# State-space steps of a hybrid encoder block: time-step matrices and squares on ScalarE, normalization one step late, the diagonal's second term in the skip weight

## The reference, cut to what matters

```python
xdt = xh * dt[..., None]
cs = jnp.cumsum(dt * a, axis=2)                      # inside a chunk of 128
seg = cs[:, :, :, None] - cs[:, :, None, :]
decay = jnp.where(mask, jnp.exp(jnp.where(mask, seg, 0.0)), 0.0)   # mask: lower triangle with diagonal
cb = jnp.einsum('bcqgn,bcsgn->bcqsg', cc, bc)
y_diag = jnp.einsum('bcqsgh,bcsghp->bcqghp', cb[..., None] * decay, xdt)
...
y = y_f + y_b + xh * d_skip[:, None]
y = y.reshape(bsz, l, SSD_INNER) * jax.nn.silu(z)
y = y.reshape(bsz, l, SSD_GROUPS, SSD_INNER // SSD_GROUPS)
y = y * lax.rsqrt(jnp.mean(y * y, -1, keepdims=True) + RMS_EPS)    # over 384 columns
y = y.reshape(bsz, l, SSD_INNER) * norm_g
return y @ w_out
```

## Time and profile before

| what | value |
|---|---|
| median of three runs | 2252.95 us (2252.62 to 2254.93) |
| profiled execution, its own time | 2250.3 us |
| its span, first to last instruction | 2248.3 us |
| busy over the span: PE, DVE, ACT, POOL | 1995.2, 674.6, 328.2, 314.7 us |
| mean granted TensorE clock | 0.94 of full |
| Sqrt of step 0 starts, Sqrt of step 14 starts | 485.20 us, 666.42 us |
| mix stage begins on TensorE | 672.70 us |

### The profile page before, as it was taken

How to read it: one execution, slowest core, us unless ns; L and a number is a source line. 1 busy time by engine, 2 the same in 40 slices (tenths; PEclk the granted TensorE clock), 3 DMA queues, 4 the chain that set the end, 5 groups by cost and what they waited for, 6 DMA issues and landing times.

```text
span 2248.3 us, 19706 instructions
## 1 busy us (share of the span) xinstructions
PE 1995.2 (89%) x8321; PEld 938.4 (42%) x8321; DVE 674.6 (30%) x1075; ACT 328.2 (15%) x547; POOL 314.7 (14%) x278
## 2 busy tenths in 40 slices
PE   8996899998979999598889889879889888988987
PEld 4664544455554444433334334334334333333332
DVE  6599965589970112300000000000000000000002
ACT  1433212144450001100000000000000000000001
POOL 2866600066640000000000000000000000000001
PEclk9898999999989999699999999999989999999999
DMA  5531221110013218389999999999999999999995
GB/s 138 126 107 26 66 96 69 39 52 28 29 57 131 84 66 351 122 341 427 429 428 424 428 428 425 431 426 427 429 427 427 428 426 427 428 427 426 427 428 228
DMA packets 86887, 625.45 MB, mean 278 GB/s; under 512 B 21036, under 2 KB 34576, under 8 KB 57616
## 3 DMA queue, kind: packets, MB, share of 16 engines
q1 hardware_dynamic: 74400, 616.41, 66.8%
q10 hardware_dynamic: 12400, 7.79, 1.2%
HBM read 614.39 MB, written 9.78 MB: 278 GB/s over the span
## 4 chain that ended last, share of the span: by engine, by line
PE 47%; DMA 28%; DVE 9%; ACT 2%; issue 1%; SPq 0%; DVEq 0%; ACTq 0%
PE ps L843 47%; DMA arena<-in_w_e 28%; ACT arena L568 1%; DVE arena L1598 1%; DVE arena L1546 1%; ACT L568 1%; DVE arena L1602 1%; DVE arena L1573 1%; DVE arena L1603 1%; DVE arena L1571 1%; DVE arena L1599 0%; DVE arena L1590 0%; DVE arena L1678 0%; DVE arena L1595 0%; DVE arena L1689 0%
## 5 line engine op out<-in xcount | busy, mean ns | idle before, releaser
L843 PE MATMUL ps<-arena 128*64 128x512 f32 (+7 forms) x7786 | 1927.6, 534 | 213.8 <-DMA arena<-in_w_e 114.5
L843 PEld LDWEIGHTS ps<-arena 128*64 128x64 f32 (+2 forms) x7786 | 877.4, 164 | 1247.8 <-issue 1062.5
L568 ACT ACTIVATE arena<-ps 128x512 f32<-128x512 f32 (+5 forms) x286 | 161.8, 597 | 1697.3 <-PE ps L843 898.2
L1698 DVE TENSOR_TENSOR arena<-arena,ps 128x512 f32<-128x512 f32 (+1 forms) x48 | 30.3, 645 | 581.5 <-PE ps L843 581.5
L560 POOL TENSOR_TENSOR arena<-arena 128x1024 f32<-128x1024 f32 x3 | 7.1, 2355 | 1324.8 <-ACT arena L568 1324.8
L1707 DVE TENSOR_TENSOR arena<-arena,ps 128x512 f32<-128x512 f32 x48 | 33.1, 690 | 338.5 <-PE ps L843 338.5
L568 ACT ACT_TABLE_LOAD x71 | 91.1, 1283 | 23.8 <-issue 21.4
L568 ACT ACTIVATE arena<-arena 64x512 f32<-64x512 f32 (+6 forms) x138 | 62.8, 513 | 164.2 <-DVE arena L1603 93.5
L1531 DVE SCALAR_TENSOR_TENSOR arena<-arena 128x512 f32<-128x512 f32 x80 | 62.5, 781 | 2.8
L1689 DVE TENSOR_TENSOR arena<-arena 128x512 f32<-128x512 f32 x8 | 5.6, 694 | 182.4 <-PE ps L1260 181.4
L544 POOL TENSOR_TENSOR arena<-arena 128x768 f32<-128x768 f32 x16 | 24.3, 1522 | 171.6 <-PE ps L1004 134.1
(11 more groups left out here) (180 smaller groups left out, 769.7 us busy)
## 6 DMA issues: line engine op xcount, KB each, us to landing
arena<-in_w_e SPq DMA_DIRECT2D x128, 2816.0 KB, 28.9
arena<-in_w_e SPq DMA_DIRECT2D x80, 2048.0 KB, 28.5
arena<-in_w_in SPq DMA_DIRECT2D x9, 2048.0 KB, 8.6
arena<-in_w_e SPq DMA_DIRECT2D x16, 1024.0 KB, 30.6
arena<-in_w_in SPq DMA_DIRECT2D x5, 1536.0 KB, 6.4
arena<-in_w_out_ssd SPq DMA_DIRECT2D x4, 1536.0 KB, 6.7
gate_scratch<-arena ACTq DMA_DIRECT2D x16, 256.0 KB, 2.4
arena<-gate_scratch SPq DMA_DIRECT2D x4, 1024.0 KB, 8.0
```

What stands on the lines that cost most here:

```text
L568: return act.activation(out, in_, func, **kw)
L843: return pe.matmul(out, lhsT, rhs, start=a, stop=z)
L1698: tt(o, o, ps[:, i, 0:w], ALU.mult).then_inc(s.hid_ready, 1)
```

## The change

Four things are done at once. (a) The time-step matrix is made by ScalarE in dt_matrix: per head one Identity of 128x128 of the mask m_gt, with scale dt_b - dt_f (dt_step, made once) and bias dt_f, both read per partition; so each side of the diagonal has its own time step and the diagonal has dt_f alone. It is double-buffered. GpSimd's three operations of a step go. (b) The missing dt_b on the diagonal is moved into the skip weight: GpSimd multiplies B and C elementwise once per group (bc_prod), TensorE sums it over the state with a column of ones (128x1 result in bank 4), and VectorE makes diag_x = dt_b * that + d_row (128x6), which replaces d_row in the skip term. (c) The squares are taken by ScalarE (Square with accum_out), and its Sqrt follows. (d) VectorE's reciprocal and scaling of step i-1 stand in step i, behind mixing_matrix(i+1).

```diff
--- before.py
+++ after.py
@@ -182,13 +182,14 @@
             return ctx.enter_context(nc.semaphore(name))
 
 
-        C = Space(arena, 0, 2300)
+        C = Space(arena, 0, 2440)
         ident, eps_col = C.take(P), C.take(1)
         late_at = C.at
         m_le, m_gt, m_ge, m_lt, ones = (C.take(P) for _ in range(5))
         chunk_no = C.take(NC)
         conv_w, conv_b = C.take(XBC // P, CONV), C.take(XBC // P)
         dt_bias, a_neg = C.take(2 * HEADS), C.take(2 * HEADS)
+        dt_step, diag_x = C.take(TT, HEADS), C.take(2, HG)
         d_row, norm_g = C.take(HEADS), C.take(INNER // P)
         dtime = C.take(TT, 2 * HEADS)
         da, w_end, e_cs, e_all = (C.take(TT, 2 * HEADS) for _ in range(4))
@@ -260,9 +261,10 @@
         cacc = S2.take(4, SEQ)
         xc = S2.take(4, SEQ)
         S = Space(arena, S.at, top)
-        dmat, uf, emat, gmat = S.take(HG, P), S.take(HG, P), S.take(HG, P), S.take(2, HG, P)
+        dmat, emat, gmat = S.take(2, HG, P), S.take(HG, P), S.take(2, HG, P)
         S = Space(arena, S2.at - 4 * SEQ, top)
         rhs_f, rhs_b = S.take(HG, P), S.take(HG, P)
+        bc_prod = S.take(SEQ)
 
 
         S = Space(arena, late_at, top)
...
@@ -538,18 +540,15 @@
             for i in range(GROUPS * TT):
                 g, c = divmod(i, TT)
                 f, b = slice(HG * g, HG * g + HG), slice(HEADS + HG * g, HEADS + HG * g + HG)
+                if c == 0:
+                    pool.wait_ge(s.silu_done, 17 + g)
+                    if g >= 1:
+                        pool.wait_ge(s.cb_ps, i)
+                    pool.tensor_tensor(bc_prod, bT[:, g, :], cT[:, g, :], ALU.mult).then_inc(s.bc_ready, 1)
                 if i >= 1:
-                    pool.wait_ge(s.mats_ready, 2 * i)
                     pool.wait_ge(s.segm_ps, i)
                 pool.tensor_tensor(rhs_f, first(m_le, HG), last(da[:, c, f], P), ALU.mult)
                 pool.tensor_tensor(rhs_b, first(m_ge, HG), last(da[:, c, b], P), ALU.mult).then_inc(s.mats_ready, 1)
-                if i == 0:
-                    pool.wait_ge(s.silu_done, 20)
-                if i >= 1:
-                    pool.wait_ge(s.g_ready, i)
-                pool.tensor_tensor(uf, first(m_le, HG), last(dtime[:, c, f], P), ALU.mult)
-                n.link(pool.tensor_tensor(dmat, first(m_ge, HG), last(dtime[:, c, b], P), ALU.mult))
-                pool.tensor_tensor(dmat, dmat, uf, ALU.add).then_inc(s.mats_ready, 1)
 
             pool.wait_ge(s.wo_ps, 2 * TT)
             pool.iota(slot_no, pattern=[[1, CAP]], base=1, channel_multiplier=0,
@@ -717,6 +716,21 @@
                     act.wait_ge(s.g_ready, i)
                 f(emat.rearrange("p (a b) q -> p a (b q)", a=2), ps[:, 2:4, 0:GI], ACT.Exp).then_inc(s.segm_exp, 1)
 
+            def dt_matrix(i):
+
+                g, c = divmod(i, TT)
+                if i >= 2:
+                    act.wait_ge(s.g_ready, i - 1)
+                for j in range(HG):
+                    h0 = HG * g + j
+                    r = f(dmat[:, i % 2, j, :], m_gt, ACT.Identity, scale=dt_step[:, c, h0:h0 + 1], bias=dtime[:, c, h0:h0 + 1])
+                r.then_inc(s.dmat_ready, 1)
+
+            def root(i):
+                act.wait_ge(s.gate_ready, i + 1)
+                n.link(f(ty[:, 0], ty[:, 3], ACT.Square, accum_out=rms[:, i % 2, 0:1]))
+                f(rms[:, i % 2, 1:2], rms[:, i % 2, 0:1], ACT.Sqrt, scale=1.0 / GI, bias=eps_col).then_inc(s.rms_sqrt, 1)
+
             def y_copied(i):
 
                 g, c = divmod(i, TT)
@@ -725,20 +739,23 @@
                     f(yT[:, 3 * g + j, P * c:P * c + P], ps[:, 1, P * j:P * (j + 1)], ACT.Copy,
                       scale=norm_g[:, 3 * g + j:3 * g + j + 1]).then_inc(s.yt_copied, 1)
 
+            act.wait_ge(s.conv_done, 20)
+            dt_matrix(0)
             z_gate(0, 0)
             decays(0)
             for c in range(1, Z_AHEAD):
                 z_gate(0, c)
+            dt_matrix(1)
             for i in range(GROUPS * TT):
                 g, c = divmod(i, TT)
                 if i + 1 < GROUPS * TT:
                     decays(i + 1)
                 if i >= 1:
                     y_copied(i - 1)
-                act.wait_ge(s.gate_ready, i + 1)
-                f(rms[:, i % 2, 1:2], rms[:, i % 2, 0:1], ACT.Sqrt, scale=1.0 / GI, bias=eps_col).then_inc(s.rms_sqrt, 1)
+                root(i)
                 if i + Z_AHEAD < GROUPS * TT:
                     z_gate(*divmod(i + Z_AHEAD, TT))
+                    dt_matrix(i + Z_AHEAD)
                 elif c == TT - 2:
 
                     act.wait_ge(s.yT5_loaded, 16)
@@ -1027,8 +1044,10 @@
                 q = slice(P * c, P * c + P)
                 if i >= 1:
                     pe.wait_ge(s.g_ready, i)
+                pe.wait_ge(s.bc_ready, g + 1)
+                mm(ps[:, 4, P:P + 1], bc_prod[:, q], ones[:, 0:1], True, True)
                 mm(ps[:, 4, 0:P], bT[:, g, q], cT[:, g, q], True, True).then_inc(s.cb_ps, 1)
-                pe.wait_ge(s.mats_ready, 2 * i + 1)
+                pe.wait_ge(s.mats_ready, i + 1)
                 if i >= 1:
                     pe.wait_ge(s.segm_exp, i)
                 for a in range(2):
@@ -1508,6 +1527,7 @@
                 if q == 0:
                     dve.wait_ge(s.seg_exp, 1)
                     n.done(tt(w_end, w_end, dtime, ALU.mult))
+                    n.done(tt(dt_step, dtime[:, :, HEADS:], dtime[:, :, 0:HEADS], ALU.subtract))
                 toeplitz_rows(q)
                 for d in range(2):
                     recur(q, d)
@@ -1568,9 +1588,21 @@
                 if i >= 2:
                     dve.wait_ge(s.yd_ps, i - 1)
                 o = gmat[:, i % 2]
+                g, c = divmod(i, TT)
+                n.done(stt(diag_x[:, i % 2], dtime[:, c, HEADS + HG * g:HEADS + HG * g + HG], ps[:, 4, P:P + 1],
+                           d_row[:, HG * g:HG * g + HG], ALU.mult, ALU.add))
                 n.link(tt(o, emat, first(ps[:, 4, 0:P], HG), ALU.mult))
-                dve.wait_ge(s.mats_ready, 2 * i + 2)
-                tt(o, o, dmat, ALU.mult).then_inc(s.g_ready, 1)
+                dve.wait_ge(s.dmat_ready, i + 1)
+                tt(o, o, dmat[:, i % 2], ALU.mult).then_inc(s.g_ready, 1)
+
+            def normalized(i):
+
+                dve.wait_ge(s.rms_sqrt, i + 1)
+                n.link(dve.reciprocal(rms[:, i % 2, 2:3], rms[:, i % 2, 1:2]))
+                if i >= 1:
+                    dve.wait_ge(s.yt_ps, i)
+                ts(ty[:, 4], ty[:, 3], rms[:, i % 2, 2:3], None, ALU.mult).then_inc(s.yn_ready, 1)
+                dve.wait_ge(s.yn_ready, i + 1)
 
             for j in range(TT - 1):
                 weighted_x(0, j)
@@ -1586,8 +1618,10 @@
                     weighted_x(g + 1, c)
                 if i + 1 < GROUPS * TT:
                     mixing_matrix(i + 1)
+                if i >= 1:
+                    normalized(i - 1)
                 y0, y1, y2 = ty[:, 0], ty[:, 1], ty[:, 2]
-                n.done(tt(h3(y0), h3(xs[:, c, gi]), bc(d_row[:, f]), ALU.mult))
+                n.done(tt(h3(y0), h3(xs[:, c, gi]), bc(diag_x[:, i % 2]), ALU.mult))
                 dve.wait_ge(s.yd_ps, i + 1)
                 if c >= 1:
                     n.done(tt(h3(y1), h3(ps[:, 6, 0:GI]), bc(e_cs[:, c, f]), ALU.mult))
@@ -1599,17 +1633,10 @@
                 tt(y0, y0, ps[:, 5, 0:GI], ALU.add).then_inc(s.y_read, 1)
                 dve.wait_ge(s.y_read, i + 1)
                 dve.wait_ge(s.z_silu, g * TT + c + 1)
-                n.link(tt(ty[:, 3], y0, zg[g % 2][:, c], ALU.mult))
-                dve.tensor_tensor_reduce(out=y0, in0=ty[:, 3], in1=ty[:, 3], scale=1.0, scalar=0.0, op0=ALU.mult, op1=ALU.add,
-                                         accum_out=rms[:, i % 2, 0:1]).then_inc(s.gate_ready, 1)
+                tt(ty[:, 3], y0, zg[g % 2][:, c], ALU.mult).then_inc(s.gate_ready, 1)
                 if more:
                     carry(g + 1, c)
-                dve.wait_ge(s.rms_sqrt, i + 1)
-                n.link(dve.reciprocal(rms[:, i % 2, 2:3], rms[:, i % 2, 1:2]))
-                if i >= 1:
-                    dve.wait_ge(s.yt_ps, i)
-                ts(ty[:, 4], ty[:, 3], rms[:, i % 2, 2:3], None, ALU.mult).then_inc(s.yn_ready, 1)
-                dve.wait_ge(s.gate_ready, i + 1)
+            normalized(GROUPS * TT - 1)
 
             dve.wait_ge(s.sg_loaded, 64)
             for hf in range(2):
```

More of the change, by code:

```diff
@@ L307, in encoder @@
         pool_step m_cleared maps_cleared xbc_ps xbc_raw conv_done silu_done nat_ps nat_copied z_ps z_silu
-        xw_ready st_ps carried cb_ps segm_ps segm_exp mats_ready g_ready yd_ps y_read gate_ready rms_sqrt
+        xw_ready st_ps carried cb_ps segm_ps segm_exp mats_ready dmat_ready bc_ready diag_ready g_ready yd_ps y_read gate_ready rms_sqrt
         yn_ready yt_ps yt_copied mix_ps mix_sig mix_read glu_done mix_ready mixT_ps mixT_copied wo_ps wo_read
```

## The result

The changed kernel takes 2289.33 us in the median (2287.83 to 2291.05, four runs) against 2252.78 of the kernel before: a ratio of 1.0161, with a 95% interval of 1.0145 to 1.0177. It is 36.5 us slower. The forecast was 18.6 slower, 2271.6, with a range up to 2286: the direction was right, the size half of what was measured, and the time lies outside the range.

What follows compares the result with a forecast made beforehand. ScalarE and VectorE handing one token back and forth bound the steps. Intervals +22.2, start -5.5, end +1.9 give +18.6 us on 2250.3, so 2268.9; plus 2.65 to the median, 2271.6 us, range 2258 to 2286.

Steps and rivals of the forecast that it cites:

- ScalarE's section: ScalarE's work from VectorE's gate_ready to the mixing matrix's start; claimed to grow from 4.32 to 8.3 us.
- The table load: Load for the Sqrt, now behind the Square and hence behind ScalarE's wait; claimed to enter the chain at 1.28 us.
- a sign against it: Named disproof in ScalarE's list: Identities taking over 0.45 or under 0.25 us each.
- My 0.07 for an operand: Cost in us of each per-partition operand of a ScalarE Identity, giving six Identities 2.05 us.
- VectorE's part: VectorE's work from mixing matrix to gate_ready: 6.55 us in chunks 1 and 2, 5.5 in chunks 0 and 3.
- TensorE's round: From L1596 to the next L1596 via transposes, z_tile, states, scores and GpSimd's pair: 14.75 us with added states, 13.4 without.
- The sum of the intervals: The 14 gate-to-gate intervals of the steps together: 203.4 us claimed against 181.2 before, +22.2.
- The circle: ScalarE and VectorE waiting on each other, gate to gate: 14.85 us eight times and 13.8 six times.
- TensorE's term: Extra from TensorE and GpSimd behind chunk 0 of groups 1 and 2: 0.9 us each, 1.8 together.
- TensorE's clock: Rival: new waits before TensorE's transposes drop z_tile to 1.2 GHz; three cases give 2287 us; chance 0.14.
- the upper bound of (3): Six Identities on ScalarE at 0.44 us each, without overlap: 2.6 us instead of 2.05.
- Start and end: Before step 0, 5.5 us gained; behind step 14, 1.9 us lost to Square and table load before the mix stage.

Runs made afterwards that it cites:

- filler run: Changed kernel plus three unused 384-column products on TensorE per step, just before it waits for the normalization: 2271.42 us, ratio 1.0082.

## Why the prediction was wrong

Set side by side, the medians make a ladder from before to after: time-step matrix and diagonal term with the Identities in ScalarE's wait, 2226.7 (two parts of the change at once, which no run separates); Identities in the section instead, 2244.9 (+18.2); squares on ScalarE, 2260.7 (+15.8); late normalization, 2289.3 (+28.7). The steps depend on their order: the last one costs 43.5 on the kernel of 2226.7, and 48 in the kernel before.

- *ScalarE's section.* Right in the main: 8.3 forecast, 8.5 measured. The table load came into the chain as read from the order. The Identities were 2.41 for six, not 2.05: each took 0.483 and followed the last by 0.39. By duration that is over the 0.45 which the prediction named as a sign against it, by pace it is not. My 0.07 for an operand came from a copy that reads PSUM and a form that reads SBUF. Both read SBUF in the Identity with two operands (0.483) and the 64x128 form with none (0.299): 0.09 for each, an estimate, as the forms differ in their partitions. The 93 ns and the some 2.3 us by the Trainium skill (ScalarE: Activation LUTs, "What ACT_TABLE_LOAD costs"), which I did not take, were nearer.
- *VectorE's part.* 7.0 and 5.7 (5.9 in chunk 3) against 6.55 and 5.5, by the filler run's chain. VectorE's products of y took 0.6 us and less, as forecast. diag_x was sized at 0.15; it takes 0.23 alone, but 0.65 in the mean, as it has two inputs in SBUF and falls under the lock, which I had tied to L1596 only.
- *The step that failed* is the one in the prediction's words: "Against ScalarE's 14.85 and 13.8 this decides only behind chunk 0 of groups 1 and 2 (14.75 against 13.8), 0.9 us each." TensorE's round was seen, but sized at full clock, 14.75 and 13.4, and so looked harmless next to the section. Its wait before the transposes was put at 1 to 2 us; it was 1.8 to 3.7. Behind ten of the 13 waits up to 686 us four to eight rows ran at half speed, some 0.3 us each. The round became 16 us and decided in most steps. The whole late normalization adds 28.4 us to the intervals (195.4 without it): 14.6 are the clock, as the filler run shows, and 13.8 are almost all VectorE's part, 0.85 to 1.1 us in most steps where 0.68 was charged.
- *The sum of the intervals, term by term.* The circle was put at 201.6 (118.8 + 82.8) and is 209.2 by the filler run: section and VectorE's part were too small by 7.6 together. TensorE's term was put at 1.8 and is 14.6, all of it gone when the clock is back. Together these are the 20 us between 203.4 and 223.75.
- *The rival "TensorE's clock"* named this and got 0.14, with "three such cases"; the clock was under 0.98 in all 14 intervals. The mistake is in the weighing: the rival was priced by how rarely it showed before, where TensorE waited for L1599 10 times, and not by the fact that the change makes the wait a fixed part of each round. The range had a slip too: the upper bound of (3) with two falls of 5.33 each comes to some 2290, not 2286.
- *A maximum of two circles at full clock* is not what a step does. In the changed kernel the weight loads waited for the scaling 13 times up to 686 us; slow rows stand behind each of the seven waits of 3.0 us and more and behind three of the six shorter ones (1.9 to 2.6), and a step whose round has slow products takes longer. I added the larger of the two for each step and nothing for what the wait does to the round. That a longer section lengthens these waits and so the slow products is likely, but not shown: with half of the Identities gone the waits were 31.1 us in 14 times instead of 35.7 in 13, and the clock stayed at 0.91.
- *Start and end.* The start gained 3.3 us against 5.5 forecast (481.93 against 485.20). From mixing matrix to gate it gained 3.4 (5.7 against 9.07), 3.2 was forecast; but the 2.3 us by which the mixing matrix was to begin earlier did not come, it begins with diag_x at 476.27 (476.13 before). The end lost 1.9, as forecast: Square of step 14 to mix 8.18, before 6.28.
- *The sum of the rest* was passed on as said. In the profile the mix stage starts 41.2 us later and the span is 41.0 longer; the medians differ by 36.5: the profiled execution of the changed kernel was 1.7 above its median, that of the kernel before 2.5 below.

What stays open: why a wait of TensorE lowers its clock in one step and not in another of the same length. In the changed kernel the wait of 1.95 us at 509.20 had one behind it (above), and this one had none:

```profile
556.43 0.31 PEld L1082 LDWEIGHTS ps<-arena 128*128 128x128 f32 x3 [1.95 <-DVE arena L1604]
556.71 12.19 PEld L860 LDWEIGHTS ps<-arena 128*128 128x128 f32 x48
```

The runs show both, not the condition.

## What to carry to other kernels

When an instruction is moved later in one engine's list, look in the lists of the others at what stands behind the wait for it: two cheap operations cost 28 to 48 us here. In large part that was because eight products that needed nothing from them stood behind the transposes that did: with these products ahead, 22.7 of 37.4 us came back. New work belongs where its engine waits anyway, ahead of the wait; six Identities cost 18 us more behind it than ahead. And a wait that comes back in every round of a TensorE loop is to be priced with the slow products behind it, not by its own length.

## What the runs showed of the hardware

Work without use made the kernel 18 us faster, with a granted clock of 0.99 instead of 0.91. VectorE's operation of 128x6 with two SBUF inputs took 0.23 us beside an idle GpSimd and up to 1.04 beside a busy one. A table load took 1.28 us, and the Sqrt behind it began 1.30 us after the load did (528.76, 530.06). A per-partition operand of an ACTIVATE costs about 0.09 us, an estimate from the Identity with two (0.483) and the form of 64x128 with none (0.299).
